# Mean squares of the head norms as two fp32r products instead of one fp32 product

## What is computed

```python
def rms_norm(x, g):
    xf = x.astype(jnp.float32)
    y = xf * lax.rsqrt(jnp.mean(xf * xf, axis=-1, keepdims=True) + NORM_EPS)
    return (y * g.astype(jnp.float32)).astype(x.dtype)

def hybrid_layer(x, mem, ...):
    h = rms_norm(x, norm_mix_g)
    proj = h @ w_in
    q_d, k_d, v_d, conv_in, q_m, gate_logits = jnp.split(proj, SPLIT_POINTS, axis=-1)
    # differential attention: 8 heads, two components of 64 each
    q = rms_norm(q_d.reshape(B, S, 8, 2, 64), q_norm_g) * 64 ** -0.5
    k = rms_norm(k_d.reshape(B, S, 8, 2, 64), k_norm_g)
    # causal softmax of both components; a = p[0] - lam * p[1]; o = a @ v
    o = rms_norm(o, subln_g) * (1.0 - lam_init)          # per head, 128 features
    y_attn = o.reshape(B, S, DIFF_WIDTH) @ w_attn_o
    # y_conv: 3-tap causal convolution between two gates, @ w_conv_o
    # y_mem: q_m as 4 heads of 256 features, rms_norm(q_m, mq_norm_g), attention to 256 memory rows
    x = x + (g0 * y_attn + g1 * y_conv + g2 * y_mem) @ w_o
    return x + jnp.square(jax.nn.relu(rms_norm(x, norm_mlp_g) @ w_mlp_in)) @ w_mlp_out
```

## Time and profile before

| | |
|---|---|
| runs | 2316.15, 2320.94, 2319.47 us; median 2319.47 |
| the profiled execution | 2320.22 us, its span (first to last instruction) 2318.5 us |
| granted TensorE clock, mean | 0.992 of full speed |
| busy: PE, PE weight loads, DVE, ACT, POOL | 98%, 81%, 61%, 38%, 9% of the span |
| the chain that ended last, by engine | PE 87%, DVE 9%, ACT 3% |
| DMA | 92 GB/s of HBM traffic over the span |

### The profile page before, as it was taken

How to read it: one execution, slowest core, us unless ns; L and a number is a source line. 1 busy time by engine, 2 the same in 40 slices (tenths; PEclk the granted TensorE clock), 3 DMA queues, 4 the chain that set the end, 5 groups by cost and what they waited for, 6 DMA issues and landing times.

```text
span 2318.5 us, 29400 instructions
## 1 busy us (share of the span) xinstructions
PE 2267.1 (98%) x10570; PEld 1876.7 (81%) x10570; DVE 1405.7 (61%) x2111; ACT 890.9 (38%) x1341; POOL 199.1 (9%) x152
## 2 busy tenths in 40 slices
PE   6999999999999999999999999999999999999999
PEld 5898788888788878888887788788887888888887
DVE  8965554454888876444446658885455657645343
ACT  4223332222477733222245535563344443322221
POOL 6402200000300030000020000002000004000000
PEclk9979999999999999999999999999999999999999
DMA  5563222222221212222222221114222122222222
GB/s 194 115 162 133 100 94 97 100 94 97 84 74 65 74 64 91 100 96 95 100 94 78 73 91 64 64 55 145 90 93 88 64 82 95 97 100 91 100 100 82
DMA packets 80132, 218.92 MB, mean 94 GB/s; under 512 B 18592, under 2 KB 28064, under 8 KB 79520
## 3 DMA queue, kind: packets, MB, share of 16 engines
q1 hardware_dynamic: 73568, 212.11, 27.1%
q10 hardware_dynamic: 6464, 5.47, 0.7%
HBM read 206.93 MB, written 6.29 MB: 92 GB/s over the span
## 4 chain that ended last, share of the span: by engine, by line
PE 87%; DVE 9%; ACT 3%; issue 1%; DMA 0%; DVEq 0%; ACTq 0%
PE lin L482 26%; PE lin L484 26%; PE lin L483 26%; PE tr L710 1%; ACT w_hi L993 1%; DVE w_lo L1422 1%; PE tr L833 1%; DVE scan L1572 0%; DVE scan L1570 0%; PE tr L601 0%; DVE scan L1575 0%; PE sc L601 0%; PE sc L697 0%; DVE sc L1557 0%; PE tr L532 0%
## 5 line engine op out<-in xcount | busy, mean ns | idle before, releaser
L993 ACT ACTIVATE w_hi<-w_raw 128x1024 fp32r<-128x1024 f32 x353 | 374.1, 1060 | 1018.8 <-PE lin L484 1007.1
L482 PE MATMUL lin<-x_hi,w_hi 128*128 128x512 f32 x1472 | 592.7, 403 | 1.8 <-DVE x_lo L1427 1.6
L484 PE MATMUL lin<-x_hi,w_lo 128*128 128x512 f32 x1472 | 573.8, 390 | 0.0
L483 PE MATMUL lin<-x_lo,w_hi 128*128 128x512 f32 x1472 | 573.2, 389 | 0.0
L1422 DVE TENSOR_TENSOR w_lo<-w_raw,w_hi 128x1024 fp32r<-128x1024 f32 x353 | 449.6, 1274 | 98.3 <-ACT w_hi L993 96.1
L482 PEld LDWEIGHTS lin<-x_hi,w_hi 128*128 128x128 f32 x1472 | 276.4, 188 | 69.5 <-issue 9.6
L483 PEld LDWEIGHTS lin<-x_lo,w_hi 128*128 128x128 f32 x1472 | 276.5, 188 | 64.5 <-issue 8.9
L484 PEld LDWEIGHTS lin<-x_hi,w_lo 128*128 128x128 f32 x1472 | 276.3, 188 | 58.4
L482 PE MATMUL lin<-q_hi,w_hi 128*128 128x512 f32 x672 | 262.7, 391 | 2.2 <-DVE w_lo L1422 2.2
L483 PE MATMUL lin<-q_lo,w_hi 128*128 128x512 f32 x672 | 262.2, 390 | 0.0
L484 PE MATMUL lin<-q_hi,w_lo 128*128 128x512 f32 x672 | 262.1, 390 | 0.0
(11 more groups left out here) (424 smaller groups left out, 2684.1 us busy)
## 6 DMA issues: line engine op xcount, KB each, us to landing
w_raw<-w SPq DMA_DIRECT2D x353, 512.0 KB, 3.2
w_raw<-w_mem SPq DMA_DIRECT2D x16, 512.0 KB, 3.9
ssm_mt<-ssm_kp SPq DMA_DIRECT2D x64, 64.0 KB, 2.7
ssm_u<-x_a SPq DMA_DIRECT2D x1, 2048.0 KB, 11.7
kv_scratch<-mem_stage SPq DMA_DIRECT2D x8, 256.0 KB, 4.4
z_b<-z_scratch SPq DMA_DIRECT2D x4, 512.0 KB, 4.3
resid<-x_b SPq DMA_DIRECT2D x1, 2048.0 KB, 10.3
out<-resid SPq DMA_DIRECT2D x8, 256.0 KB, 2.1
```

The source lines that it names most:

```text
L482: nc.tensor.matmul(out, WH[:, b, w], xh[:, k, 0:cols], start=(k == 0), stop=False)
L483: nc.tensor.matmul(out, WH[:, b, w], xl[:, k, 0:cols], start=False, stop=False)
L484: last = nc.tensor.matmul(out, WL[:, b, w], xh[:, k, 0:cols], start=False, stop=(k == KC - 1))
L993: nc.scalar.activation(WH[:, b, :], raw[:, r, :], ACT.Copy).then_inc(s_hi, 1)
```

## The change

1. The constant matrices `ones` and `ones64` become fp32r (built by POOL in a scratch area and copied); where the others need `ones` as fp32, it is read as such.
2. Each head norm's square is made twice by ScalarE: rounded to fp32r (`sq_hi`, `sq_hi_b`, `head_sq_hi`) and in fp32 (`sq`, `sq_b`). The rest, `sq - sq_hi`, is an fp32r tensor `sq_lo`: by VectorE for queries and keys, by POOL for the heads and the memory queries. TensorE does two products with the constant, on the high and on the low part.
3. Queries and keys run in one loop of 16 (`query_keys`), with four value buffers, two sets of squares and two banks in turn. Product pair i stands in slab i+1 ahead of chunk 7; pairs 0 and 1 in slab 2 ahead of chunk 5 and slab 3 ahead of chunk 2. The instructions on ScalarE and VectorE are put in another order.
4. Memory queries (`mem_queries`): each pair ahead of chunk 7 of the next slab.
5. Heads: the product moves from behind the second scores to conv 0 of the next head, ahead of chunk 2. On ScalarE the root and half square come behind the second component's exponentials.

```diff
+def mean_at(i):
+    return (2 * KC + 5, 3 * KC + 2)[i] if i < 2 else KC * (i + 1) + KC - 1
...
+    onesr, bo64 = sm("ones", [P], F32R), sm("ones64", [P], F32R)
+    onesd = onesr[:].bitcast(F32)
...
+    SQL = at("sq_lo", 198 * KB, [L], F32R)
...
-                def means(i):
-                    pe.wait_ge(s_sq, c.up(s_sq))
-                    out = AUX if i != 1 or ready is None else TR[0]
-                    nc.tensor.matmul(out[:, 0:cols], ones[:], SQ[:, 0:cols],
-                                     start=i % group == 0, stop=i % group == group - 1).then_inc(s_ms, 1)
...
+            def qk_sums(out, hi, lo):
+                pe.wait_ge(s_sqh, c.up(s_sqh, 2))
+                pe.wait_ge(s_sq, c.up(s_sq))
+                nc.tensor.matmul(out[:], bo64[:], hi[:], start=True, stop=False)
+                nc.tensor.matmul(out[:], bo64[:], lo[:], start=False, stop=True).then_inc(s_ms, 1)
+
+            def square_sums(out, ones, hi, start=True, stop=True):
+                pe.wait_ge(s_sqh, c.up(s_sqh, 2))
+                nc.tensor.matmul(out[:], ones[:], hi[:], start=start, stop=False)
+                pe.wait_ge(s_sq, c.up(s_sq))
+                nc.tensor.matmul(out[:], ones[:], SQL[:], start=False, stop=stop).then_inc(s_ms, 1)
...
+            def query_keys(ready, before_last):
+                for n in range(QK):
+                    mids = {mean_at(i) % KC: qk_mean(i) for i in range(QK) if mean_at(i) // KC == n}
+                    if n == 1:
+                        mids[3] = final_mean_squares
+                    if n == QK - 1:
+                        before_last()
+                    linear(Slab(FIRST["dif_q"] + n, n, None, 0), XH, XL, mid=mids, ready=None if n else ready)
+                return {mean_at(QK - 1) % KC: qk_mean(QK - 1)}
...
             for h in range(DH):
-                for i in range(2):
-                    linear(Slab(FIRST["conv"] + 3 * h + i, 3 * h + i, None, 0), XH, XL, mid=tail if h + i == 0 else None)
+                linear(Slab(FIRST["conv"] + 3 * h, 3 * h, None, 0), XH, XL, mid=head_mean_square if h else tail, mid_at=2 if h else 3)
+                linear(Slab(FIRST["conv"] + 3 * h + 1, 3 * h + 1, None, 0), XH, XL)
...
-                if h + 1 < DH:
-                    head_mean_square()
...
@@ ScalarE @@
+            def query_keys(before_last):
+                split_hi(Slab(FIRST["dif_q"] + 1, 1, None, 0))
+                qk_squares(0)
+                qk_squares(1)
+                qk_root(0)
+                qk_squares(2)
+                split_hi(Slab(FIRST["dif_q"] + 2, 2, None, 0))
+                qk_hi(0)
+                qk_root(1)
+                qk_hi(1)
+                for n in range(3, QK):
+                    if n == QK - 1:
+                        before_last()
+                    qk_root(n - 1)
+                    qk_squares(n)
+                    split_hi(Slab(FIRST["dif_q"] + n, n, None, 0))
+                    qk_hi(n - 1)
...
                 if h:
                     causal_exps(D_E[1], 1)
-                if h:
+                    root_and_half_square(ACC[:], AUX[:], T2[:], 2 * HD)
                     dif_out(h - 1)
...
-                nc.scalar.activation(SQ[:], TR[0][:], ACT.Square).then_inc(s_sq, 1)
-                root_and_half_square(ACC[:], AUX[:], T2[:], 2 * HD)
+                nc.scalar.activation(HSQH[:], TR[0][:], ACT.Square).then_inc(s_sqh, 1)
+                nc.scalar.activation(SQ[:], TR[0][:], ACT.Square).then_inc(s_sqh, 1)
+            root_and_half_square(ACC[:], AUX[:], T2[:], 2 * HD)
...
@@ VectorE @@
+                for n in range(3, QK):
+                    if n == QK - 1:
+                        before_last()
+                    query_evac(first + n, MBUF[n % 4])
+                    qk_lo(n - 2)
+                    qk_norm(n - 1)
+                    qk_square_lo(n)
+                    split_lo(Slab(first + n, n, None, 0))
...
@@ POOL @@
+            def square_lo(hi):
+                pool.wait_ge(s_sqh, c.up(s_sqh, 2))
+                g_.tensor_tensor(SQL[:], SQ[:], hi[:].bitcast(F32), ALU.subtract).then_inc(s_sq, 1)
```

197 lines of the change are left out of this document (122 added, 75 removed).

## The result

The changed kernel took 2301.41 us (median of 8 runs, 2300.09 to 2303.43), the kernel before 2319.66 us beside it (8 runs, 2308.68 to 2329.09): ratio 0.9925, 95% interval 0.9902 to 0.9948. The profiled execution after took 2301.41 us, 18.8 less than that of before, where 9.5 had been forecast.

The account below looks back on a forecast made before the run. TensorE, busy for 98% of the span, was taken to set the end. From the profiled 2320.2 us, -9.5 (queries, keys), -3.1 (memory queries) and +3.1 (heads) gave 2310.7, less 0.75 for the median: 2310.0 us, range 2304.5 to 2316.5.

Parts of the forecast that it names:

- Price of a product: Each mean-square product on TensorE: fp32 costs 0.86 us, the new fp32r pair 0.46, saving 0.41; 32 such products.
- rival E: The pair runs no faster than the fp32 product, 13 us less gain: 2323 us; chance 0.03.
- Queries and keys: Query and key slabs: 16 x 0.41 saved, 5.6 us of idleness removed, 2.7 of new waits: 9.5 us gained.
- C: Rival: the steady query slab's 0.4 us isn't there, 11 slabs lose 4.4 us: 2314.4 us; chance 0.16.
- D: Rival: query slab 4's lateness never heals, each of 11 slabs waits 1.3 us: 2324 us; chance 0.06.
- The two waits of the ends: New TensorE waits: 1.3 us with the restart at an early query pair, 0.65 at the pair in the first value slab.
- Heads: Convolution-stage heads: 1.1 us lost to the ring, 0.15 gained at the first, 2.1 lost at the last: 3.1 us lost.
- the ring: Heads: a closed chain through norm, probabilities, filter, squares, exponentials and root sets each head at 25.80 us, against 25.62 now.
- Rival B: The heads' ring does not bind, so they lose nothing or gain up to 3 us: 2306 us; chance 0.18.
- Memory queries: Eight pairs save 3.3 us, two short waits of 0.35 go, three new stalls of 0.3: 3.1 us gained.
- The constants' two copies on POOL lie in front of 17.8 us of idle TensorE: nothing.: Kernel start: POOL's two copies of the constants were claimed to cost nothing.
- Nothing else moves: Everything outside queries, keys, heads and memory queries was claimed to stay as profiled, with no term in the sum.

Follow-up runs that it names:

- v2a: e6's kernel with each head's mean square as one fp32 product of the whole square inside the next slab, no GpSimd in the heads: 2300.0 us.
- v2b: v2a with VectorE making the probabilities ahead of the last head's norm: 2293.16 us.
- the repeat: The changed kernel run again with nothing altered, 12 runs: 2309.64 us.
- both further runs: Two more single runs of the unaltered changed kernel, each with a trace: 2309.54 and 2311.64 us.
- e2: The changed kernel with its constants set at the start as before and rounded to fp32r by POOL later: 2308.14 us.
- e4: The changed kernel with POOL's product into d_diag waiting for the fourth power table instead of the second: 2309.21 us.
- e6: e2's kernel with the first product of the SSM tables computed three times, 2.5 us more VectorE work: 2302.3 us.
- e10: e6's kernel with half its delay, the first table product computed twice instead of three times: 2301.39 us.
- the second further run: The second of two extra traced runs of the unaltered changed kernel: 2311.64 us.
- e1: The kernel before with only the constants built as in the changed kernel, copied by POOL into fp32r tiles: 2315.08 us.
- v1: e6's kernel with the heads' pair in front of chunk 4 instead of chunk 2 and the probabilities ahead of the norm: 2291.91 us.
- v4: v1 with the last head's mean square as one fp32 product of its whole square: 2290.52 us.
- e3: The changed kernel with the heads as before: one fp32 product, root ahead of the second exponentials, no GpSimd there: 2312.04 us.
- e5: The kernel before with the first product of the SSM tables computed three times, 2.5 us more VectorE work: 2319.89 us.

## Why the prediction was right and where it was wrong

**Price of a product: right.** Timeline of TensorE in a steady query slab after (as the earlier trace rows):

```profile
1263.31 0.39 PE L501 MATMUL lin<-x_hi,w_lo 128*128 128x512 f32 x1
1263.54 0.39 PE L848 MATMUL tr<-sq_hi_b,ones 128*128 128x512 f32 x1
1263.76 0.39 PE L849 MATMUL tr<-sq_lo_b,ones 128*128 128x512 f32 x1
1263.99 0.39 PE L499 MATMUL lin<-x_hi,w_hi 128*128 128x512 f32 x1
```

Two steps, 0.45 us, so 0.41 is saved; rival E falls.

**Queries and keys: right**, 9.0 us for 9.5, and 9.0 in the thirteen other traces with the new loop too. Steady slabs start 5.89 us apart (forecast 5.92) without a wait, so C and D fall. The two waits of the ends are there, where and as long as worked out (1.3 with the restart and 0.65):

```profile
1239.85 0.47 PE L848 MATMUL tr<-sq_hi_b,ones 128*128 128x512 f32 x1 [1.09 <-DVE sq_lo_b L1934]
...
1313.97 0.47 PE L848 MATMUL tr<-sq_hi_b,ones 128*128 128x512 f32 x1 [0.77 <-DVE sq_lo_b L1934]
```

**Heads: the ring right, the sum partly by luck.** In this pair 2.9 us are lost for 3.1. The ring was worked out at 25.80 us and is 25.79; each low product waits for POOL, and the last head for two squares and POOL:

```profile
1412.89 0.50 PE L856 MATMUL tr<-sq_lo,ones 128*128 128x512 f32 x1 [0.86 <-POOL sq_lo L2274]
...
1438.68 0.50 PE L856 MATMUL tr<-sq_lo,ones 128*128 128x512 f32 x1 [0.86 <-POOL sq_lo L2274]
...
1564.51 0.50 PE L854 MATMUL tr<-head_sq_hi,ones 128*128 128x512 f32 x1 [0.73 <-ACT sq L1381]
1565.86 0.50 PE L856 MATMUL tr<-sq_lo,ones 128*128 128x512 f32 x1 [0.84 <-POOL sq_lo L2274]
```

Rival B falls, and v2a and v2b show the mechanism. POOL's subtraction took 1.27 us for the 1.29 taken. But up to the last head's values 1.5 us are lost where the sum had 0.95, and behind them 1.3 where it had 2.1: two errors that cancel. And this trace is the exception. In the seven other traces with these heads (the repeat, both further runs, e2, e4, e6, e10) the clock falls behind the last head's two waits, here in the second further run:

```profile
1572.00:1578.00 6.00, 4.42 (x12) 3.01 (x11) 1.88 (x4) 2.37 (x5) 1.27 (x1) 0.74 0.19 74
```

There 3.0 us are lost behind the last values and the heads lose 4.5 in all. The sum held no such term.

**Memory queries: right in the sum**, 3.5 us for 3.1, with another instruction held up. POOL's subtractions were not longer (1.29 to 1.33 us). In the first three norms of after it was VectorE's last gain product, with two inputs in SBUF, that took 1.78 or 1.79 us beside them where an undisturbed one took 0.75. Ahead of the first memory scores TensorE lost about 0.2 us twice by it; the sum had three times 0.3. The first of them:

```profile
1761.71 0.75 DVE L1919 SCALAR_TENSOR_TENSOR t<-t,cols,acc 128x512 f32<-128x512 f32 x1
1762.38 1.78 DVE L1919 SCALAR_TENSOR_TENSOR val<-val,cols,acc 128x512 f32<-128x512 f32 x1
...
1762.29 1.32 POOL L2274 TENSOR_TENSOR sq_lo<-sq,sq_hi 128x512 fp32r<-128x512 f32 x1 [5.08 <-ACT sq L1304]
```

**"The constants' two copies on POOL lie in front of 17.8 us of idle TensorE: nothing. Nothing else moves": wrong, and "Nothing else moves" is the step that failed.** The sum took everything ahead of the queries over from the profiled run of before, at its times, with no term for it and no reason but the idle TensorE. In the pair of traces that stretch gave 9.3 us, as much as the change itself: TensorE's wait of 3.47 us at the outflow was gone, and with it a clock of 0.50 for 24 us (the 9.3 us are net of the shorter early falls). How much of this the change itself brings isn't shown. The copies do move VectorE's start: its first 128x64 product (L1594) starts at 19.05 to 19.22 in the eight traces with copies at the start and at 18.79 to 18.82 in the ten without; in the profiled pair its squaring loop starts at 18.69 for 18.27. But e1, with the copies alone, gained nothing in the median. Whether they make the lower group more frequent is not settled: 13 runs of 22 with them, 7 of 24 in e2 and e4 without the meeting, 2 of 12 in e1. That a start later by 1.2 to 2.5 us makes it nearly certain is shown: 37 of the 39 runs of e6, e10, v1, v2a, v2b and v4 have it.

**The second fault is in the numbers, not in the steps:** the forecast took the profiled run's group for the kernel's time. The three runs shown spread over 4.8 us, half of the gain that I forecast, and the profiled run had 24 us at 0.50 in its trace. Group against group the change is worth 7.0 us (median 2308.45 to 2301.41 in the lower group) to 7.7 (2317.5 to 2309.8 in the next), and the traces agree: 9.0 - 4.5 + 3.5 = 8.0 us with the last head's fall of the clock, for the 9.5 forecast. The rest of the 18.3 us between the two medians of the result is the group. (The chances of the direction were added up a little wrong: they are 0.83 faster and 0.09 slower.)

**An effect that I didn't see and that favours the change:** the clock of the old heads fell to 0.5 to 0.6 behind their waits in some runs (11 us in e3, 10 in e5). Of the 61 runs with the pair behind POOL (after, e2, e4, e6, e10) none is above 2311.7, while e5, e3 and before have runs above that, and the traces of e3 and e5 show such falls in the heads. Why a wait of 0.86 us in the first seven heads has no fall behind it, the last head's 0.73 and 0.84 in a row have one in seven of eight traces, and one of 0.73 in front of an fp32 product has one in some runs, stays open.

## What to carry to other kernels

Where TensorE is busy for 98% of the span, look through the granted clock in windows of a few us before summing terms: behind the waits of 1.1 us and more at the outflow the clock halved for up to 24 us, so that their cost was not their length. Forecast such a kernel by groups of runs, not by one profiled run, and ask of each shift of the start which wait it makes or fills. A ring is broken by taking a step whose result is wanted later (here the norm of the last head) from in front of the step that others wait for; here it gave 0.44 us a head without falls of the clock (25.30 to 24.86), 0.77 with the one fall, and the cheaper product in place of the fp32 one 0.45.

## What the runs showed of the hardware that I had not expected

Adding work can make a stretch faster: in e5's trace, with 2.5 us more on VectorE, the first mean square came 10.3 us earlier than in before's, most of it through the clock, though e5's median did not gain. e6, with the same work added, took 2302.3 us where the changed kernel on the same occasion took 2309.64. A wait of 1.1 us of TensorE was followed by 1.2 GHz in the SSM stage just as one of 3.5 us was, while one of 2.0 us near 42 us, in the second further run, was followed by a clock of 1.00. The same 0.73 us wait in front of the same fp32 product was followed by 1.2 GHz for some 4 us in one run (two passes in 2.07 us) and by nothing in another (1.13 us). A VectorE instruction of 0.22 us took 1.83 us because POOL's 1.92 us instruction had started 0.18 us ahead of it.
